# Four PSUM banks for the matrix-building products of a PEER layer, and two weight loads put behind the V rows

## The chip, the cores and the metric

The kernel runs on one NeuronCore of a Trainium2 chip. The time is device microseconds of one execution; what is compared is the median over several runs. Everything is float32 in memory.

## The reference, cut to what matters

Two layers over 256 tokens of width 2048: layer 0 is an mLSTM mixer, layer 1 grouped-query attention, and each is followed by a PEER mixer. The change lies in PEER and in the first load behind it.

```python
def peer(xn, wq, k1, k2, u, v):
    ...                                    # 8 heads, 16 experts each: idx and gate, (tokens, 128)
    def block(args):                       # 2 blocks of 128 tokens
        x_blk, i_blk, g_blk = args
        act = gelu(einsum('td,ted->te', x_blk, u[i_blk]))
        return einsum('te,ted->td', g_blk * act, v[i_blk])

for layer in range(2):
    h = rms_norm(x, ln_mix[layer])
    x = x + (mlstm_mixer, attn_mixer)[layer](h, ...)
    h = rms_norm(x, ln_ffn[layer])
    x = x + peer(h, ...)
```

There are 16384 experts, numbered as 128 x 128. So the second einsum reads, for each token, 128 rows of the table v.

## The kernel before

**PEER's second einsum is done in two ways at once.** Columns 1024 to 2047 of v are gathered: for each token block and each pick p, one indirect DMA brings 128 rows (one per token, 4 KB each, 512 KB in all) and VectorE adds them, scaled, to x (`add_value`, L2001). Columns 0 to 1023 are done dense: `experts_W[b]` is a matrix with, for each expert row e and each token, the weight of the picks on expert (e, partition); 128 expert rows times 2 blocks times 2 banks make 512 matmuls a layer of 128x128 by 128x512 (`dense`, L1433), which gather in PSUM banks acc[0] to acc[3]. The table's half comes in 64 "vd pairs" of 1 MB each, through three slots (`load_dense`, L551, on SP's queue).

**Picks brought forward.** Block 0's first 40 picks are gathered ahead of time ("rows ahead", POOL L631). TensorE adds each with two matmuls against a diagonal matrix (L1418) into acc[0] and acc[1]; VectorE moves these sums to x (L2059) before the dense matmuls of block 0 use the banks. The other gathers (L672, "V rows") are 216 a layer, `G_ALL`, through six slots. The gathers with j under 2 wait for the indices, those with j of 2 and 3 and the vd pair 2 for the last row ahead, and from j = 4 on for the last group of block 1's build.

**The build of `experts_W`.** For each block there are 32 groups of four tokens. For a token t the product of two 128x128 matrices, one-hot by one-hot times weight, gives a 128x128 piece (L1408). Four pieces fill one PSUM bank; TensorE uses `mis[0]` and `mis[1]` in turn. ScalarE copies the bank out (L922). Before group `done` TensorE waits for the copy of the group two before:

```python
if done >= 2:
    pe.wait_ge(wb_out, done - 1)
for j in range(GROUP):
    last = mm(mis[g % 2][:, j * P:(j + 1) * P], onehot_2[g % DEPTH[b]][:, j, :], ...
```

Block 0's build runs beside the dot products with u: ScalarE makes all its selectors (L903) and takes one group at a time. Block 1's build stands by itself, after the last dot product and before the dense phase. In it VectorE makes the weighted selectors of every group (L1981) and the one-hot selectors of the even ones (L1985), ScalarE the one-hot ones of the odd groups (L912, L915); both lie in four buffers, and the selectors of group g wait until group g - 4 is done. ScalarE's order is written out: copies of g and g + 1 (g even), then the selectors for g + 5. Behind the groups 4, 8, ... 24 TensorE adds one row ahead each. I call four groups with one row ahead a round.

**The loads behind.** In layer 0 SP's queue holds, in order, the 64 vd pairs and, put behind the pairs 28, 36, 44 and 52, the four quarters (1 MB each) of the next layer's key weights, chunk 16 of 26 (L510). These go to the arena, where expert rows already used have left room, and VectorE and ScalarE split the first three into two parts between the V rows (L455, L461). Then come the quarters 0 and 1 of chunk 17: quarter 0 into `ring[10]`, once vd pair 62 is used (`vd_used` at 63), quarter 1 into `ring[11]`, a slot of the V rows, once all V rows are added. ScalarE's queue has, behind the build, the load of the next norm's gain (L709, 1 MB), three casts of key quarters, the squares of both x blocks (L721, they wait for all V rows and for the bank sums, L2071), the cast of the fourth quarter and then the casts of the transposed x (L427), on which chunk 16's matmuls wait.

The names of PSUM: eight banks of 512 floats a partition, `acc` = banks 0 to 3, `trb` = 4 and 5 (transposes), `mis` = 6 and 7. acc[2] and acc[3] take block 1's dense sums, and before that mixer chunks.

Of the kernel before, what the change touches and what calls it, by code (L numbers as in the profile page):

```python
# [19 lines left out]
P = 128  # L20
# [68 lines left out]
def trunk_kernel(nc, consts, x, ln_mix, ln_ffn, m_w_in, m_gate_bias, m_head_norm, m_w_out,  # L89
# [13 lines left out]
    CH = 512  # L103
# [9 lines left out]
    with ExitStack() as ctx:  # L113
# [63 lines left out]
        acc, trb, mis = banks[0:4], banks[4:6], banks[6:8]  # L177
# [10 lines left out]
        w_landed = [sem(f"w_landed{j}") for j in range(4)]  # L188
# [29 lines left out]
        wb_full, wb_out = sem("wb_full"), sem("wb_out")  # L218
# [91 lines left out]
        GROUP = 4  # L310
# [8 lines left out]
        spread += [rows_1[:, i * CH:(i + 1) * CH].rearrange("p (t e) -> p t e", e=P) for i in range(4)]  # L319
        onehot_2, weighted_1 = spread[0::2], spread[1::2]  # L320
        DEPTH = [2, 4]

        def wait_spread(eng, l, b, g):

# [181 lines left out]
        def _(sp):  # L506
# [35 lines left out]
            def load_dense(l):  # L542

                for p in range(D_PAIRS):
                    if p == 0:
                        sp.wait_ge(dot_done, (l + 1) * LAYER_TILES)
                    if p == 2:
                        sp.wait_ge(ahead_used, (l + 1) * N_AHEAD)
                    if p >= ND:
                        sp.wait_ge(vd_used, l * D_PAIRS + p - ND + 1)  # L550
                    sp.dma_start(d_slot[p % ND], vd_tab[l][p]).then_inc(vd_landed[p % ND], 16)  # L551
                    if l == 0 and p in KEYS_BEHIND:
                        j = KEYS_BEHIND.index(p)
                        sp.wait_ge(vd_used, 24 + 8 * j)
                        load_quarter(a_w_in[0], slice(4 * CH, 5 * CH), w_raw(16, j), j, keys_landed)
                        sp.sem_inc(w_landed[j], 16)

            KEYS_BEHIND = [28 + 8 * j for j in range(4)]
            load_quarter(m_w_in[0], slice(0, CH), ring[0], 0)
            sp.dma_start(xb[0][:, CH:D], x[0, 0:P, CH:D]).then_inc(x_in[0], 16)  # L560
            sp.dma_start(gain[:, CH:D], ln_mix[0, CH:D].partition_broadcast(P)).then_inc(gain_in, 16)
# [8 lines left out]
            for i, g in enumerate((a_q_norm, a_k_norm)):  # L570
                sp.dma_start(qkgain[:, i * P:(i + 1) * P], g[0].partition_broadcast(P)).then_inc(qkg_in, 16)
            load_dense(0)
            sp.wait_ge(vd_used, D_PAIRS - 1)
            load_quarter(a_w_in[0], slice(5 * CH, 6 * CH), w_raw(17, 0), 0)
            sp.wait_ge(vg_added, G_ALL)
# [126 lines left out]
        def _(act):  # L702
# [151 lines left out]
            def peer(l):  # L854
# [63 lines left out]
                def weights_group(b, g):  # L918

                    act.wait_ge(wb_full, (2 * l + b) * GROUPS + g + 1)  # L920
                    dst = experts_W[b].rearrange("p (q t r) -> p t q r", t=P, r=RUN)[:, GROUP * g:GROUP * (g + 1)]
                    copy(dst, mis[g % 2][:, :].rearrange("p (t q r) -> p t q r", t=GROUP, r=RUN)).then_inc(wb_out, 1)  # L922

                def diagonal(v):

# [176 lines left out]
        def _(pe):  # L1102
# [281 lines left out]
            def peer(l):  # L1384
# [9 lines left out]
                def weights_group(b, g):  # L1394

                    done = (2 * l + b) * GROUPS + g
                    if b == 0:
                        pe.wait_ge(onehot_act, l * (GROUPS + GROUPS // 2) + g + 1)
                    elif g % 2:
                        pe.wait_ge(onehot_act, l * (GROUPS + GROUPS // 2) + GROUPS + g // 2 + 1)  # L1400
                    else:
                        pe.wait_ge(onehot_dve, l * (GROUPS // 2) + g // 2 + 1)
                    if b:
                        pe.wait_ge(weighted_ready, l * GROUPS + g + 1)
                    if done >= 2:
                        pe.wait_ge(wb_out, done - 1)
                    for j in range(GROUP):
                        last = mm(mis[g % 2][:, j * P:(j + 1) * P], onehot_2[g % DEPTH[b]][:, j, :],  # L1408
                                  weighted_1[g % DEPTH[b]][:, j, :],
                                  start=True, stop=True, skip_group_check=True)  # L1410
                    last.then_inc(wb_full, 1)
# [872 lines left out]
```

## Time and profile before

| | us |
|---|---|
| median of 3 runs | 3179.17 (3179.15 to 3181.28) |
| the profiled execution's own time | 3180.36 |
| its span in the profile | 3178.5 |
| TensorE busy | 2229.8 (70%) |
| VectorE busy | 2446.9 (77%) |
| ScalarE busy | 813.8 (26%) |
| GpSimd busy | 1631.3 (51%) |
| DMA | 1096.33 MB, mean 345 GB/s |

How to read it: the rows come from one profiled execution; times are microseconds from the span's start. PE is TensorE's matmuls, PEld its weight loads, DVE VectorE, ACT ScalarE, POOL GpSimd, SPq SyncE's queue. A row of the timeline has the start, the time, the engine, the line of the kernel, the operation, what is written and read, the shapes and a count (xN: neighbouring instructions merged); in brackets the engine's idle time before it and what ended that. A float32 product stands as two records, so x8 is one group and x4 with 128x512 one row ahead. A matmul's end is modelled and overlaps the start of the next.

### The profile page before, as it was taken

To read this page: it belongs to the slowest core of one execution; us is meant where nothing else is said; L and a number is where in the kernel's file an instruction comes from. 1 tells how busy PE (TensorE), PEld (TensorE's weight loads), DVE (VectorE), ACT (ScalarE), POOL (GpSimd) and SP (SyncE) were. 2 spreads that over 40 slices of the span, in tenths; PEclk is the share of its full clock that TensorE was granted. 3 is DMA by queue.
4 is the path that set the end of the run, shared out by engine and by line. 5 is a ranking of instruction groups with operands and counts; after the bars stand their busy time and mean duration, and the time that the engine had idled before them with its cause. 6 is when DMAs were issued, how large, how long until landed. Compare 5 with 4: busy or idle time off the path is not lost.

```text
span 3178.5 us, 23916 instructions
## 1 busy us (share of the span) xinstructions
PE 2229.8 (70%) x7748; PEld 1627.4 (51%) x7748; DVE 2446.9 (77%) x3513; ACT 813.8 (26%) x1773; POOL 1631.3 (51%) x1051
## 2 busy tenths in 40 slices
PE   7999983452134369999989999454213335999999
PEld 6887772341122146666658877343112223666666
DVE  4454579999999986666665767999999998666665
ACT  4344410000345572000003442000025556300000
POOL 1000036657788845655550103556878885365664
PEclk9999996775566679999999999766656767999999
DMA  6554589999999968999984437999999997699998
GB/s 233 179 191 141 181 342 407 421 402 402 417 420 420 420 273 326 413 413 413 412 348 146 159 113 306 405 421 404 413 401 420 420 420 317 263 413 411 413 413 363
DMA packets 231210, 1096.33 MB, mean 345 GB/s; under 512 B 23208, under 2 KB 23984, under 8 KB 144176
## 3 DMA queue, kind: packets, MB, share of 16 engines
q0 software_dynamic: 147456, 805.37, 62.3%
q1 hardware_dynamic: 80256, 282.22, 23.4%
q10 hardware_dynamic: 3376, 7.23, 0.7%
q8 instruction: 62, 1.02, 0.1%
q14 instruction: 60, 0.49, 0.0%
HBM read 1092.63 MB, written 2.11 MB: 344 GB/s over the span
## 4 chain that ended last, share of the span: by engine, by line
PE 34%; DVE 30%; DMA 18%; issue 9%; POOL 7%; ACT 2%; ACTq 0%; SPq 0%; DVEq 0%; POOLq 0%
DVE ring_sb L2027 19%; PE bank L1142 15%; PE bank L1433 14%; DMA actT_sb<-in_peer_vg_dram,idx_all 8%; DMA ring_sb<-in_peer_u_dram,idx_all 6%; POOL ring_sb L655 5%; DMA ring_sb<-in_peer_vg_dram,idx_all 3%; DVE x_sb L2001 1%; PE bank L1408 1%; POOL actT_sb L672 1%; DVE shared L1740 1%; DVE shared L1736 1%; DVE pair_all L1744 1%; PE bank L1418 1%; ACT ring_sb L922 1%
## 5 line engine op out<-in xcount | busy, mean ns | idle before, releaser
L655 POOL DMA_INDIRECT ring_sb<-in_peer_u_dram,idx_all x496 | 889.1, 1792 | 345.1 <-DVE idx_all L1745 203.0
L2027 DVE CUSTOM_DVE_ANT_0 ring_sb<-ring_sb,arena 128x2048 f32<-128x2048 f32 x256 | 574.5, 2286 | 21.9 <-DMA ring_sb<-in_peer_u_dram,idx_all 20.7
L2027 DVE CUSTOM_DVE_ANT_0 ring_sb<-ring_sb,actT_sb 128x2048 f32<-128x2048 f32 x256 | 573.2, 2285 | 13.5 <-DMA ring_sb<-in_peer_u_dram,idx_all 13.1
L2001 DVE SCALAR_TENSOR_TENSOR x_sb<-actT_sb,gate_rows,x_sb 128x1024 f32<-128x1024 f32 x288 | 369.1, 1284 | 222.0 <-DMA actT_sb<-in_peer_vg_dram,idx_all 215.0
L1142 PE MATMUL bank<-w_parts,actT_hi 128*128 128x512 f32 x1664 | 520.8, 394 | 7.3 <-DVE w_parts L461 5.2
L1433 PE MATMUL bank<-ring_sb 128*128 128x512 f32 x1024 | 481.6, 592 | 1.4 <-ACT ring_sb L922 1.4
L1433 PE MATMUL bank<-ring_sb,arena 128*128 128x512 f32 x1024 | 481.3, 593 | 0.4 <-DMA ring_sb<-in_peer_vd_dram 0.4
L672 POOL DMA_INDIRECT actT_sb<-in_peer_vg_dram,idx_all x288 | 349.1, 1212 | 249.0 <-DVE x_sb L2001 190.3
L1408 PE MATMUL bank<-gain 128*128 128x128 f32 x768 | 144.6, 348 | 413.0 <-ACT gain L903 386.9
L1189 PE MATMUL bank<-arena 128*128 128x256 f32 x896 | 249.7, 445 | 233.4 <-DVE shared L2027 233.4
L461 DVE TENSOR_TENSOR w_parts<-ring_sb,w_parts 128x2048 fp32r<-128x2048 f32 x100 | 228.7, 2292 | 212.1 <-ACT w_parts L455 212.1
L1408 PEld LDWEIGHTS bank<-gain 128*128 128x128 f32 x768 | 126.4, 248 | 481.6 <-ACT gain L903 439.0
L1433 PEld LDWEIGHTS bank<-ring_sb,arena 128*128 128x128 f32 x1024 | 301.5, 295 | 139.1 <-DMA ring_sb<-in_peer_vd_dram 2.1
L1433 PEld LDWEIGHTS bank<-ring_sb 128*128 128x128 f32 x1024 | 301.3, 294 | 139.2 <-ACT ring_sb L922 1.7
L1142 PEld LDWEIGHTS bank<-w_parts,actT_hi 128*128 128x128 f32 x1664 | 310.5, 189 | 72.7 <-issue 9.4
L1189 PEld LDWEIGHTS bank<-arena 128*128 128x128 f32 x896 | 200.1, 227 | 280.5 <-DVE shared L2027 245.8
L2001 DVE SCALAR_TENSOR_TENSOR x_sb<-ring_sb,gate_rows,x_sb 128x1024 f32<-128x1024 f32 x144 | 184.3, 1284 | 106.6 <-DMA ring_sb<-in_peer_vg_dram,idx_all 100.8
L1418 PE MATMUL bank<-ring_sb,keysT 128*128 128x512 f32 x272 | 185.8, 825 | 112.4 <-ACT keysT L932 101.8
L455 ACT CAST w_parts<-ring_sb 128x2048 fp32r<-128x2048 f32 x100 | 190.6, 1909 | 273.1 <-DMA ring_sb<-in_mlstm_w_in_dram 134.4
L672 POOL DMA_INDIRECT ring_sb<-in_peer_vg_dram,idx_all x144 | 181.5, 1260 | 152.7 <-DVE x_sb L2001 78.5
L1142 PE MATMUL bank<-w_parts,actT_lo 128*128 128x512 f32 x640 | 249.7, 390 | 0.0
L631 POOL DMA_INDIRECT ring_sb<-in_peer_vg_dram,idx_all x80 | 150.0, 1876 | 78.3 <-PE bank L1418 56.7
(217 smaller groups left out, 2081.1 us busy)
## 6 DMA issues: line engine op xcount, KB each, us to landing
ring_sb<-in_peer_vd_dram SPq DMA_DIRECT2D x128, 1024.0 KB
ring_sb<-in_mlstm_w_in_dram SPq DMA_DIRECT2D x48, 1024.0 KB, 5.1
arena<-in_peer_wq_dram SPq DMA_DIRECT2D x28, 1024.0 KB, 13.7
ring_sb<-in_attn_w_in_dram SPq DMA_DIRECT2D x20, 1024.0 KB, 5.1
ring_sb<-in_mlstm_w_out_dram SPq DMA_DIRECT2D x16, 1024.0 KB, 5.1
ring_sb<-in_attn_w_out_dram SPq DMA_DIRECT2D x16, 1024.0 KB, 5.0
ring_sb<-in_peer_u_dram,idx_all POOLq DMA_INDIRECT x496, 12.8
actT_sb<-in_peer_vg_dram,idx_all POOLq DMA_INDIRECT x288
```

Source lines behind the costliest of these rows:

```text
L455: nc.scalar.copy(w_hi_of[j], w_raw(c, j)).then_inc(w_hi, 1)
L461: nc.vector.tensor_tensor(w_lo_of[j], w_raw(c, j), w_hi_of[j].bitcast(F32), ALU.subtract).then_inc(w_lo[j], 1)
L631: nc.gpsimd.indirect_dma_start(out=ahead_slot[v % 4], out_offset=None, in_=vg_tab[l], in_offset=bass.IndirectOffsetOnAxis(ap=idx_all[0][:, ...
L655: nc.gpsimd.indirect_dma_start(out=ring[i % NU], out_offset=None, in_=u_tab[l], in_offset=bass.IndirectOffsetOnAxis(ap=rows_at, axis=0),). ...
L672: nc.gpsimd.indirect_dma_start(out=g_slot[G_SLOT[j]], out_offset=None, in_=vg_tab[l], in_offset=bass.IndirectOffsetOnAxis(ap=idx_all[b][:, ...
L1142: last = mm(acc[2 * par + b][:, :], xp, wp, start=(j == 0 and k == 0 and i == 0), stop=(j == 3 and k == QK - 1 and i == 2), skip_group_che ...
L1189: last = mm(mis[0][:, side * T:(side + 1) * T], slots[half][:, k % 8, side * P:(side + 1) * P], yT[:, k, :], start=(k == 0), stop=(k == KT ...
L1408: last = mm(mis[g % 2][:, j * P:(j + 1) * P], onehot_2[g % DEPTH[b]][:, j, :], weighted_1[g % DEPTH[b]][:, j, :], start=True, stop=True, s ...
L1418: last = mm(acc[n][:, :], diag_of(v), ahead_slot[v % 4][:, n * CH:(n + 1) * CH], start=(v == 0), stop=(v == N_AHEAD - 1), skip_group_check ...
L1433: last = mm(acc[2 * b + n][:, :], experts_row(b, e), d_slot[p % ND][:, i * DENSE + n * CH:i * DENSE + (n + 1) * CH], start=(e == 0), stop= ...
L2001: v.scalar_tensor_tensor(out=xb[b][:, DENSE:D], in0=g_slot[G_SLOT[j]], scalar=w_all[b][:, p:p + 1], in1=xb[b][:, DENSE:D], op0=ALU.mult, o ...
L2027: v.tensor_tensor_reduce(ring[i % NU], ring[i % NU], rows[b], 1.0, 0.0, ALU.mult, ALU.add, dots[u % 2][:, k:k + 1]).then_inc(dot_done, 1)
```

## The change

A list `built` of four banks takes the place of `mis[g % 2]`: mis[0], mis[1], acc[2], acc[3], and TensorE waits for the copy of the group four before. In layer 0 the last key quarter is no longer put behind vd pair 52 but behind all pairs, and it waits there until 214 of the 216 V rows are added. The first quarter of chunk 17 stands behind it in the same queue, and so behind that wait.

```diff
--- before.py
+++ after.py
@@ -319,6 +319,7 @@
         spread += [rows_1[:, i * CH:(i + 1) * CH].rearrange("p (t e) -> p t e", e=P) for i in range(4)]
         onehot_2, weighted_1 = spread[0::2], spread[1::2]
         DEPTH = [2, 4]
+        built = [mis[0], mis[1], acc[2], acc[3]]
 
         def wait_spread(eng, l, b, g):
 
@@ -555,7 +556,7 @@
                         load_quarter(a_w_in[0], slice(4 * CH, 5 * CH), w_raw(16, j), j, keys_landed)
                         sp.sem_inc(w_landed[j], 16)
 
-            KEYS_BEHIND = [28 + 8 * j for j in range(4)]
+            KEYS_BEHIND = [28 + 8 * j for j in range(3)]
             load_quarter(m_w_in[0], slice(0, CH), ring[0], 0)
             sp.dma_start(xb[0][:, CH:D], x[0, 0:P, CH:D]).then_inc(x_in[0], 16)
             sp.dma_start(gain[:, CH:D], ln_mix[0, CH:D].partition_broadcast(P)).then_inc(gain_in, 16)
@@ -570,6 +571,10 @@
             for i, g in enumerate((a_q_norm, a_k_norm)):
                 sp.dma_start(qkgain[:, i * P:(i + 1) * P], g[0].partition_broadcast(P)).then_inc(qkg_in, 16)
             load_dense(0)
+            sp.wait_ge(vg_added, G_ALL - 2)
+            sp.wait_ge(vd_used, 24 + 8 * 3)
+            load_quarter(a_w_in[0], slice(4 * CH, 5 * CH), w_raw(16, 3), 3, keys_landed)
+            sp.sem_inc(w_landed[3], 16)
             sp.wait_ge(vd_used, D_PAIRS - 1)
             load_quarter(a_w_in[0], slice(5 * CH, 6 * CH), w_raw(17, 0), 0)
             sp.wait_ge(vg_added, G_ALL)
@@ -919,7 +924,7 @@
 
                     act.wait_ge(wb_full, (2 * l + b) * GROUPS + g + 1)
                     dst = experts_W[b].rearrange("p (q t r) -> p t q r", t=P, r=RUN)[:, GROUP * g:GROUP * (g + 1)]
-                    copy(dst, mis[g % 2][:, :].rearrange("p (t q r) -> p t q r", t=GROUP, r=RUN)).then_inc(wb_out, 1)
+                    copy(dst, built[g % 4][:, :].rearrange("p (t q r) -> p t q r", t=GROUP, r=RUN)).then_inc(wb_out, 1)
 
                 def diagonal(v):
 
@@ -1402,10 +1407,10 @@
                         pe.wait_ge(onehot_dve, l * (GROUPS // 2) + g // 2 + 1)
                     if b:
                         pe.wait_ge(weighted_ready, l * GROUPS + g + 1)
-                    if done >= 2:
-                        pe.wait_ge(wb_out, done - 1)
+                    if done >= 4:
+                        pe.wait_ge(wb_out, done - 3)
                     for j in range(GROUP):
-                        last = mm(mis[g % 2][:, j * P:(j + 1) * P], onehot_2[g % DEPTH[b]][:, j, :],
+                        last = mm(built[g % 4][:, j * P:(j + 1) * P], onehot_2[g % DEPTH[b]][:, j, :],
                                   weighted_1[g % DEPTH[b]][:, j, :],
                                   start=True, stop=True, skip_group_check=True)
                     last.then_inc(wb_full, 1)
```

## Rows read from the trace of the kernel before

**Rows 1.** The page, part 2: granted clock and DMA share in 40 slices.

```profile
PEclk9999996775566679999999999766656767999999
DMA  6554589999999968999984437999999997699998
```

**Rows 2.** Busy time by stage: both layers' builds and dense phases.

```profile
core 0: us, PE busy (x) PEld busy (x) DVE busy (x) ACT busy (x) POOL busy (x), PEclk, DMA share, GB/s
1159.26:1212.24 52.98, 43.29 (x280) 35.82 (x280) 46.31 (x144) 43.78 (x108) 6.38 (x7) 0.97 0.27 97
1212.24:1653.21 440.97, 440.58 (x1024) 301.31 (x1024) 274.75 (x214) 5.70 (x3) 260.61 (x212) 1.00 1.02 408
...
2682.45:2735.43 52.98, 44.28 (x280) 36.85 (x281) 46.16 (x143) 43.45 (x107) 6.16 (x7) 0.95 0.27 95
2735.43:3175.27 439.84, 439.84 (x1024) 301.46 (x1024) 274.65 (x217) 0.00 (x0) 262.25 (x212) 1.00 1.00 402
```

**Rows 3.** The timeline at layer 1's end: start us, us, engine, line, instruction.

```profile
3165.45 2.67 DVE L2001 SCALAR_TENSOR_TENSOR x_sb<-actT_sb,gate_rows,x_sb 128x1024 f32<-128x1024 f32 x2 [0.69 <-DMA actT_sb<-in_peer_vg_dram,idx_all]
...
3173.39 1.88 PE L1433 MATMUL bank<-ring_sb 128*128 128x512 f32 x4
```

**Rows 4.** The timeline at layer 0's end, VectorE and ScalarE.

```profile
1655.50 1.28 DVE L2001 SCALAR_TENSOR_TENSOR x_sb<-ring_sb,gate_rows,x_sb 128x1024 f32<-128x1024 f32 x1 [1.68 <-DMA ring_sb<-in_peer_vg_dram,idx_all]
1657.10 2.67 DVE L2001 SCALAR_TENSOR_TENSOR x_sb<-actT_sb,gate_rows,x_sb 128x1024 f32<-128x1024 f32 x2 [0.32 <-DMA actT_sb<-in_peer_vg_dram,idx_all]
...
1664.87 1.88 ACT L455 CAST w_parts<-arena 128x2048 fp32r<-128x2048 f32 x1
...
1668.63 0.58 ACT L427 CAST actT_hi<-bank 128x512 fp32r<-128x512 f32 x1 [1.88 <-PE bank L1115]
```

**Rows 5.** ScalarE's timeline behind it, the next chunk's first cast.

```profile
1692.05 3.72 ACT L455 CAST w_parts<-ring_sb 128x2048 fp32r<-128x2048 f32 x2
```

**Rows 6.** The timeline of one round of the build, layer 0.

```profile
1176.47 0.59 ACT L922 COPY ring_sb<-bank 128x512 f32<-128x512 f32 x1 [1.13 <-PE bank L1408]
...
1179.50 1.13 PE L1408 MATMUL bank<-gain 128*128 128x128 f32 x8 [1.18 <-ACT ring_sb L922]
...
1180.47 1.88 PE L1418 MATMUL bank<-ring_sb,shared 128*128 128x512 f32 x4
1180.67 1.11 DVE L1981 TENSOR_SCALAR gain<-const,shared 128x128 f32<-128x128 f32 x4 [0.43 <-PE bank L1408]
...
1181.58 0.57 ACT L922 COPY ring_sb<-bank 128x512 f32<-128x512 f32 x1
...
1183.08 2.06 PE L1408 MATMUL bank<-actT_sb 128*128 128x128 f32 x16
1183.28 0.59 ACT L922 COPY ring_sb<-bank 128x512 f32<-128x512 f32 x1 [1.13 <-PE bank L1408]
1183.28 1.12 DVE L1981 TENSOR_SCALAR gain<-const,shared 128x128 f32<-128x128 f32 x4 [0.90 <-PE bank L1408]
```

**Rows 7.** TensorE's timeline: starts of the two builds, and layer 0's last four groups.

```profile
1159.26 3.54 PE L1408 MATMUL bank<-gain 128*128 128x128 f32 x16 [2.37 <-DVE gain L1985]
...
1165.87 1.13 PE L1408 MATMUL bank<-gain 128*128 128x128 f32 x8 [1.18 <-ACT ring_sb L922]
...
1206.76 2.02 PE L1408 MATMUL bank<-gain 128*128 128x128 f32 x16 [1.18 <-ACT ring_sb L922]
...
2682.20 3.78 PE L1408 MATMUL bank<-gain 128*128 128x128 f32 x16 [2.38 <-DVE gain L1985]
2685.78 3.09 PE L1408 MATMUL bank<-actT_sb 128*128 128x128 f32 x16
2689.06 1.13 PE L1408 MATMUL bank<-gain 128*128 128x128 f32 x8 [0.19 <-ACT ring_sb L922]
```

**Rows 8.** The DMA issues by line, last column the median us to landing.

```profile
ring_sb<-in_attn_w_in_dram SPq DMA_DIRECT2D x20, 1024.0 KB, 5.1
...
arena<-in_attn_w_in_dram SPq DMA_DIRECT2D x4, 1024.0 KB, 15.9
```

## The prediction

> **What bounds the kernel now.** I read first the profile by slices [rows 1]: the DMA share stands at 9 over two long stretches, and the granted clock is low in between. These stretches are the V phases of the two PEER layers. Then I cut each layer's end into stages [rows 2]. The build of block 1's expert matrix takes 52.98 us, and in it TensorE is busy for 43.29 us, VectorE 46.31, ScalarE 43.78: nobody is full, so they wait for each other. The dense phase behind it takes 440.97 us in layer 0 and 439.84 in layer 1. TensorE is full in it, and so are the DMA engines (share 1.02 and 1.00): two streams side by side, the matmuls with their vd pairs, and the gathered V rows that VectorE adds.
>
> Which of the two ends last differs. In layer 1 the last V row is added at 3165.45 + 2.67 = 3168.12, the last matmul ends at 3173.39 + 1.88 = 3175.27: TensorE ends the layer by 7.15 us [rows 3]. In layer 0 TensorE ends at 1653.21 [rows 2], and the last row is added at 1657.10 + 2.67 = 1659.77 [rows 4]: the V rows end the layer, by 6.56 us. Nothing of what comes next (squares, norm, transposes) starts before that.
>
> **Inside the build.** One round of four groups (16 products of 128x128) and one row ahead [rows 6]. TensorE: a pause of 1.18 us that ends with ScalarE's copy, a group 0.97 (1179.50 to 1180.47), the row ahead and the next group 2.61 (to 1183.08), two groups 2.06: 5.64 us of work in a round of 6.81 (ScalarE's copy at 1176.47 to the next such copy at 1183.28). ScalarE: from 1176.47 to 1181.58 + 0.57 = 1182.15 without a pause, 5.68 us, then 1.13 us idle until TensorE. VectorE waits 0.43 us here and 0.90 at 1183.28, both for TensorE, so it works 5.48. TensorE waits for the copy of the group two before; ScalarE then waits for the group that came late. All three need under 5.7 us; with two banks the round takes 6.81.
>
> **Part 1, four banks in block 1's build.** Group g now waits for the copy of group g - 4. In ScalarE's order the copies of groups 4m and 4m+1 are behind it when TensorE has finished 4m+3, so the pause of 1.18 us goes. No instruction is added: 128 products and 32 copies a layer as before. What is late next is ScalarE's own work, 5.68 us, with TensorE's 5.64 beside it. VectorE's selectors for group g + 4 need only that group g is done, and 5.48 fits. I take 5.75 us a round, a little over the longest of the three; the bounds are 5.68 (no loss) and 6.2 (half of the pause comes back, since three queues in order with nearly the same load can't all run without a gap). From group 4 (1165.87) to group 28 (1206.76) there are six rounds [rows 7]: 6 x 1.06 = 6.4 us. The first round has one pause of that kind, 1.18, before group 4; the queues have only just filled there, so I take 0.7 of it. The last one, 1206.76 to 1212.24 = 5.48 us, becomes two pairs of groups of 2.02 and a copy of 0.57, with the hand-overs about 4.7: 0.7. Layer 0: **7.8 us**, bounds 4.5 and 9.1. In layer 1 the build takes 53.23 us (2682.20 to 2735.43), and its first four groups run at the low clock, 3.78 and 3.09 us for a pair, so that the first pause is 0.19 and not 1.18 [rows 7]: **7.2 us**, bounds 4.0 and 8.1.
>
> Here a page speaks against. The granted clock is 0.97 and 0.95 in the builds [rows 2], that is the high level (2.4 GHz) but for their start, in spite of a pause every round; so I count nothing for the clock. The Trainium skill, "TensorE: Matmul & The Clock Gate", section "A second HAM failure mode: psum-queue depth-cycling", says that a kernel cycling through banks left TensorE small pauses and made its clock swing; by it the build would gain less than the sum or lose. The trace does not agree for two banks, and four take pauses away. It is the last rival.
>
> Block 0's build is paced by ScalarE's selectors, made between the dot products; in its order the copy of group g - 2 stands ahead of the selectors of g. So TensorE never waited for a bank there: zero, and if that cover were gone it would be a gain. Banks 2 and 3 are idle in the build (rows ahead gather in 0 and 1; dense matmuls into 2 and 3 wait for all copies, as they did): zero.
>
> **What the earlier end is worth.** Layer 1: dense phase and V rows both start behind the build, TensorE is without a gap for 439.84 us and ends the layer; all 7.2 us count. Layer 0: the gathers from j = 4 on wait for the last group, the two before and the third vd pair for the last row ahead, both in the build; the V stream moves as a whole, 7.8 us.
>
> **Part 2, two megabytes behind the V rows (layer 0).** Moved are two loads on SP's queue, 1 MB each. The last key quarter leaves its place behind pair 52 and passes 11 vd pairs (53 to 63). The next chunk's first quarter, which waited for vd pair 63 and so went out one pair, 440.97 / 64 = 6.9 us, ahead of TensorE's end, now waits for the last-but-two V row too. The two layers tell what a megabyte costs. Against layer 1, layer 0 carries six more in this phase: the gain for the next norm, four key quarters, the first quarter of chunk 17. Its V rows end 6.56 us behind TensorE, layer 1's 7.15 us ahead: 13.7 / 6 = 2.28 us each. The DMA engines at about 408 GB/s give 1.05 MB / 0.408 = 2.57 us. Two of them out of the V rows' way: **4.6 us**. The row end would stand 2.0 us behind TensorE's, so the V rows still bound the layer; the gain can't pass 6.56 us. The lower bound is 2.0: near the end VectorE adds rows back to back at 1.33 us (two in 2.67) [rows 4] and no free DMA speeds that up. The adds at 1655.50 and 1657.10 waited 1.68 and 0.32 us for their landings, so there is something to win there.
>
> What it could cost. SP now stands at the wait for V row 214; queued behind are only the quarters of chunk 17, the first cast of which is at 1692.05 [rows 5]. The key quarter goes out when row 214 is added, 1655.50 + 1.28 = 1656.78 in the old times. ScalarE casts it at 1664.87, behind the two squares, and the first cast that anybody waits for comes at 1668.63; so it may land until 1668.63 - 1.88 = 1666.75, that is 9.9 us after issue. Median landings are 5.1 us for such loads on a quiet queue and 15.9 for the key quarters in the middle of the dense phase [rows 8]. At 1656.78 the matmuls' loads are over and two V rows are left, so I take a value near 5.1, at most 8: zero cost. If it were 15.9, 6.0 us would be lost.
>
> **The sum.** 7.8 + 7.2 + 4.6 = 19.6 us, on the profiled execution: 3180.4 - 19.6 = 3160.8 us (the span from 3178.5 to 3158.9). The median of the runs lies 1.2 us lower: 3179.2 - 19.6 = **3159.6 us**.
>
> **Rivals.**
> (a) The build gains about half: a round of 6.2, since ScalarE's order (two copies, then a set of selectors) holds up TensorE in another place. For it: three loads of 5.5 to 5.7 us; against: four banks are a slack of a whole round. 4.5 + 4.0 + 4.6 = 13.1: 3166.1 us. Chance 0.12.
> (b) The V rows don't follow the freed megabytes, VectorE being their bound near the end. For it: adds back to back from 1657.10; against: the comparison of the layers. 15.0: 3164.2 us. Chance 0.12.
> (c) The key quarter lands late (15.9 us) and holds up chunk 16: 19.6 - 6.0 = 13.6: 3165.6 us. Chance 0.05.
> (d) The change does not what it says: the bank was only one of two waits that ended together, and TensorE now stops for a selector as long as for the copy. 4.6 us are left: 3174.6 us, no change. Chance 0.03.
> (e) Slower: the clock falls in the build. The first pair of groups at the low level (1.2 GHz) took 3.54 us against 2.02 for a late pair [rows 7], and a stream without pauses would double: 5.64 becomes 11.3, 5.5 us over the 5.75. With four or more of the sixteen rounds low, the 19.6 us are eaten; with all of them it is 16 x 5.5 = 88, some 3248 us. Nothing in the trace shows it: chance 0.02.
>
> **How the numbers follow.** The forecast has 0.66. Its best end is 9.1 + 8.1 + 6.6 = 23.8: 3155.4 us. Its poor end and the rivals (a), (b), (c) lie at up to 3166.1. With half a microsecond to one at either side for the scatter of runs, the range is 3154.5 to 3167. A difference under 0.2%, 6.4 us, can't be told from none: faster 0.95, same 0.03 (d), slower 0.02 (e).
>
> **What would show it.** Right: rounds of 5.7 to 5.8 us and no pause of TensorE for the copy at 1.18; the builds 45 and 46 us long; layer 0's last V row 2 us behind TensorE's last matmul; the key quarter's cast straight behind the squares, with no wait for a DMA; layer 1's dense phase still 440 us. Wrong: a new wait of TensorE for selectors; V rows still 6 us behind; ScalarE waiting for the key quarter; a clock under 1.00 in the middle of a build.

## The result, and the profile after

The changed kernel takes 3158.7 us (median of 4 runs, 3157.0 to 3161.9) against 3179.2 us: 20.5 us less, ratio 0.9931 (95% interval 0.9919 to 0.9942). Forecast were 3159.6. A second set of five runs (e11) gave 0.9922 (0.9909 to 0.9936). The profiled span fell from 3178.5 to 3156.6 us, by 21.9; forecast were 19.6. In the new file the line numbers are up to five higher: the build's products L1413 (were L1408), the copy L927 (L922), the V rows L2006 (L2001), the dense matmuls L1438 (L1433). The files of the experiments differ from this by a few lines again.

First the busy time by stage, the changed kernel (columns as in [rows 2]): the builds and the dense phases of the two layers.

```profile
1160.78:1205.28 44.50, 42.20 (x281) 35.51 (x281) 44.40 (x143) 42.96 (x108) 6.74 (x7) 0.95 0.33 114
1205.28:1647.46 442.18, 442.16 (x1024) 301.47 (x1024) 282.25 (x221) 6.04 (x4) 260.73 (x212) 1.00 1.02 408
2668.71:2713.53 44.82, 42.54 (x280) 35.86 (x281) 44.72 (x144) 42.90 (x108) 6.07 (x7) 0.94 0.33 115
2713.53:3153.37 439.84, 439.84 (x1024) 301.47 (x1024) 275.75 (x217) 0.00 (x0) 268.96 (x212) 1.00 1.00 402
```

The builds take 44.50 and 44.82 us, where they took 52.98 and 53.23 (from the first product to the first dense matmul). TensorE, VectorE and ScalarE are busy for 42.20, 44.40 and 42.96 us, a little less than before (43.29, 46.31 and 43.78), in a time that is 8.5 us shorter. VectorE's 44.40 of 44.50 us is not all selectors: it has made the last of them 3.7 us before the build's end, and goes on with the sums of the rows ahead and the first V rows. Layer 1's dense phase is 439.84 us, as before.

Next TensorE's timeline in layer 0's build, a round in the middle and then the end of the build.

```profile
1177.01 1.06 PE L1413 MATMUL bank<-gain 128*128 128x128 f32 x8
1177.90 1.88 PE L1423 MATMUL bank<-ring_sb,shared 128*128 128x512 f32 x4
1179.62 1.05 PE L1413 MATMUL bank<-gain 128*128 128x128 f32 x8
1180.51 1.95 PE L1413 MATMUL bank<-actT_sb 128*128 128x128 f32 x16
1182.30 1.06 PE L1413 MATMUL bank<-gain 128*128 128x128 f32 x8
...
1200.55 1.16 PE L1413 MATMUL bank<-gain 128*128 128x128 f32 x8 [0.74 <-ACT gain L920]
...
1203.34 1.16 PE L1413 MATMUL bank<-actT_sb 128*128 128x128 f32 x8 [0.74 <-ACT actT_sb L920]
1205.28 3.40 PE L1438 MATMUL bank<-ring_sb 128*128 128x512 f32 x4 [0.78 <-ACT ring_sb L927]
```

and one round of ScalarE's, from an odd group's selectors to those of the group four later:

```profile
1176.24 1.28 ACT L917 ACTIVATE gain<-const,shared 128x128 f32<-128x128 f32 x4
...
1181.82 1.28 ACT L917 ACTIVATE gain<-const,shared 128x128 f32<-128x128 f32 x4
```

A round is 1182.30 - 1177.01 = 5.29 us and has no pause; [rows 6] had 6.81 with 1.18 of pause. ScalarE's round is 1181.82 - 1176.24 = 5.58 us, and from the second group's copy on it never waits again, so it sets the length of the build: TensorE runs ahead of it at 5.29 us a round and from group 20 on goes at 5.58 too. Only at the end does TensorE wait, 0.74 us twice for ScalarE's selectors (L920) and 0.78 for the last copy.

Then layer 0's end, SyncE's queue, VectorE, ScalarE and TensorE.

```profile
1643.07 0.38 SPq L511 DMA_DIRECT2D arena<-in_attn_w_in_dram  x1
1643.15 2.67 DVE L2006 SCALAR_TENSOR_TENSOR x_sb<-actT_sb,gate_rows,x_sb 128x1024 f32<-128x1024 f32 x2
...
1643.57 56.74 SPq L511 DMA_DIRECT2D ring_sb<-in_attn_w_in_dram  x7
...
1645.74 2.48 DVE L2076 TENSOR_TENSOR x_sb<-bank,x_sb 128x512 f32<-128x512 f32 x4
...
1650.91 1.88 ACT L456 CAST w_parts<-arena 128x2048 fp32r<-128x2048 f32 x1
...
1653.53 1.97 PE L1120 MATMUL bank<-const,arena 128*128 128x128 f32 x8 [6.06 <-DVE arena L1642]
1654.68 0.58 ACT L428 CAST actT_hi<-bank 128x512 fp32r<-128x512 f32 x1 [1.88 <-PE bank L1120]
```

and chunk 16's first transposes in the kernel before:

```profile
1667.48 1.75 PE L1115 MATMUL bank<-const,arena 128*128 128x128 f32 x7 [14.27 <-DVE arena L1637]
```

The last V row is added at 1643.15 + 2.67 = 1645.82, 440.54 us after the dense phase's start; before, it was 447.53 [rows 2, 4]. TensorE's last matmul ends at 1647.46: the V rows, 6.56 us late before, are 1.64 us ahead. The key quarter goes out at 1643.07 and is cast at 1650.91 right behind the squares, with no wait for it. TensorE starts on chunk 16's transposes 6.06 us after its last dense matmul, where it was 14.27.

It is still the V rows that release what follows. From the last V row's add to chunk 16's transposes it is 1653.53 - 1645.82 = 7.71 us, and before 1667.48 - 1659.77 = 7.71; all thirteen profiles have 7.70 or 7.71, also the four in which TensorE ends later than the last row (by 1.64 us here, 0.83, 0.17 and 0.05 in e10, e8 and e4). Behind the last V row VectorE adds the four bank sums (L2076), and only the fourth needs TensorE's last matmul: it begins some 1.7 us after the last V row's end (an estimate from the 2.48 us of the four), and in layer 0 no profile shows a wait there. In layer 1 each of the four waits for TensorE:

```profile
3153.41 0.69 DVE L2076 TENSOR_TENSOR x_sb<-bank,x_sb 128x512 f32<-128x512 f32 x1 [0.17 <-PE bank L1438]
```

So in layer 0 TensorE may end up to about 1.7 us behind the last V row before that costs anything, and the change uses 1.64 of them.

By stage, before to after, in us:

| stage | before | after | change |
|---|---|---|---|
| start to layer 0's build | 1159.26 | 1160.78 | +1.5 |
| build, layer 0 | 52.98 | 44.50 | -8.5 |
| dense phase, layer 0 | 440.97 | 442.18 | +1.2 |
| its end to chunk 16 | 14.27 | 6.07 | -8.2 |
| chunk 16 to layer 1's build | 1014.72 | 1015.18 | +0.5 |
| build, layer 1 | 53.23 | 44.82 | -8.4 |
| dense phase, layer 1 | 439.84 | 439.84 | 0 |
| the rest | 3.23 | 3.23 | 0 |

The first line is scatter: nothing there was changed, and the eleven later profiles have it between 1159.1 and 1163.9. The +1.2 is told of at the end; with the -8.2 below it, it makes the 7.0 us by which the last V row comes sooner after the dense phase's start.

### The profile page after: what moved, and what is told of

Read it like the earlier page. It is cut to its first block, busy times and chain, and to the rows that moved or that the text cites. A ratio compares the mean times of both kernels' runs of the same rounds, so it can differ in the third digit from the quotient of the medians.

```text
span 3156.6 us, 23915 instructions
## 1 busy us (share of the span) xinstructions
PE 2231.8 (71%) x7748; PEld 1630.4 (52%) x7748; DVE 2445.7 (77%) x3513; ACT 812.1 (26%) x1773; POOL 1639.5 (52%) x1051
## 4 chain that ended last, share of the span: by engine, by line
PE 33%; DVE 30%; DMA 18%; issue 8%; POOL 7%; ACT 3%; ACTq 0%; SPq 0%; DVEq 0%; POOLq 0%
DVE ring_sb L2032 20%; PE bank L1147 15%; PE bank L1438 14%; DMA actT_sb<-in_peer_vg_dram,idx_all 7%; DMA ring_sb<-in_peer_u_dram,idx_all 6%; POOL ring_sb L660 5%; DMA ring_sb<-in_peer_vg_dram,idx_all 3%; DVE x_sb L2006 2%; ACT ring_sb L927 1%; POOL actT_sb L677 1%; DVE shared L1745 1%; DVE shared L1741 1%; DVE pair_all L1749 1%; POOL ring_sb L636 1%; PE bank L1357 0%
## 5 line engine op out<-in xcount | busy, mean ns | idle before, releaser
L2032 DVE CUSTOM_DVE_ANT_0 ring_sb<-ring_sb,arena 128x2048 f32<-128x2048 f32 x256 | 574.4, 2285 | 21.6 <-DMA ring_sb<-in_peer_u_dram,idx_all 20.3
L2032 DVE CUSTOM_DVE_ANT_0 ring_sb<-ring_sb,actT_sb 128x2048 f32<-128x2048 f32 x256 | 573.4, 2285 | 14.2 <-DMA ring_sb<-in_peer_u_dram,idx_all 13.7
L2006 DVE SCALAR_TENSOR_TENSOR x_sb<-actT_sb,gate_rows,x_sb 128x1024 f32<-128x1024 f32 x288 | 369.0, 1284 | 217.3 <-DMA actT_sb<-in_peer_vg_dram,idx_all 214.1
L1438 PE MATMUL bank<-ring_sb 128*128 128x512 f32 x1024 | 482.9, 594 | 1.5 <-ACT ring_sb L927 1.5
L1438 PE MATMUL bank<-ring_sb,arena 128*128 128x512 f32 x1024 | 481.7, 593 | 0.0
L677 POOL DMA_INDIRECT actT_sb<-in_peer_vg_dram,idx_all x288 | 359.3, 1248 | 233.2 <-DVE x_sb L2006 171.7
L1413 PE MATMUL bank<-gain 128*128 128x128 f32 x768 | 146.1, 351 | 398.6 <-ACT gain L908 386.7
L462 DVE TENSOR_TENSOR w_parts<-ring_sb,w_parts 128x2048 fp32r<-128x2048 f32 x100 | 228.6, 2291 | 214.0 <-ACT w_parts L456 214.0
L1438 PEld LDWEIGHTS bank<-ring_sb,arena 128*128 128x128 f32 x1024 | 301.6, 295 | 139.6 <-issue 1.5
L1438 PEld LDWEIGHTS bank<-ring_sb 128*128 128x128 f32 x1024 | 301.3, 294 | 139.9 <-ACT ring_sb L927 1.9
L1413 PEld LDWEIGHTS bank<-gain 128*128 128x128 f32 x768 | 129.0, 252 | 464.6 <-ACT gain L908 437.3
L2006 DVE SCALAR_TENSOR_TENSOR x_sb<-ring_sb,gate_rows,x_sb 128x1024 f32<-128x1024 f32 x144 | 184.6, 1284 | 102.4 <-DMA ring_sb<-in_peer_vg_dram,idx_all 101.0
```

The costliest lines, as they stand in the source:

```text
L462: nc.vector.tensor_tensor(w_lo_of[j], w_raw(c, j), w_hi_of[j].bitcast(F32), ALU.subtract).then_inc(w_lo[j], 1)
L677: nc.gpsimd.indirect_dma_start(out=g_slot[G_SLOT[j]], out_offset=None, in_=vg_tab[l], in_offset=bass.IndirectOffsetOnAxis(ap=idx_all[b][:, ...
L1413: last = mm(built[g % 4][:, j * P:(j + 1) * P], onehot_2[g % DEPTH[b]][:, j, :], weighted_1[g % DEPTH[b]][:, j, :], start=True, stop=True, ...
L1438: last = mm(acc[2 * b + n][:, :], experts_row(b, e), d_slot[p % ND][:, i * DENSE + n * CH:i * DENSE + (n + 1) * CH], start=(e == 0), stop= ...
L2006: v.scalar_tensor_tensor(out=xb[b][:, DENSE:D], in0=g_slot[G_SLOT[j]], scalar=w_all[b][:, p:p + 1], in1=xb[b][:, DENSE:D], op0=ALU.mult, o ...
L2032: v.tensor_tensor_reduce(ring[i % NU], ring[i % NU], rows[b], 1.0, 0.0, ALU.mult, ALU.add, dots[u % 2][:, k:k + 1]).then_inc(dot_done, 1)
```

## The experiments

Each is compared with the kernel before on the same chip, where that took 3181.1 us (e1 to e4), 3181.6 (e5 to e8) and 3182.2 (e9 to e11). "V end" below is the time from the start of layer 0's dense phase to the last V row's add, read from each profile's timeline. It repeats well: 447.5 and 447.7 us in the two profiles with both loads among the V rows and nothing else moved (before, e1), 440.4 to 441.0 in the six with both loads behind them (the change, e2, e3, e4, e8, e11).

### e1 and e2: one part alone

e1 is the changed kernel with both loads where they were:

```diff
-            KEYS_BEHIND = [28 + 8 * j for j in range(3)]
+            KEYS_BEHIND = [28 + 8 * j for j in range(4)]
...
             load_dense(0)
-            sp.wait_ge(vg_added, G_ALL - 2)
-            sp.wait_ge(vd_used, 24 + 8 * 3)
-            load_quarter(a_w_in[0], slice(4 * CH, 5 * CH), w_raw(16, 3), 3, keys_landed)
-            sp.sem_inc(w_landed[3], 16)
```

> Four banks, both loads where they were before. The changed kernel's builds took 44.5 and 44.8 us instead of 53.0 and 53.2, its V rows ended 7.0 us earlier against the start of the dense phase. Theory 1 (the builds are worth 16.9 us whatever the loads do, the 7.0 us belong to the two megabytes): builds of 44.5 to 45 us, the last V row of layer 0 again 6.6 us behind TensorE's last matmul, 3162 us. Rival (part of the 7.0 us comes from the build, since four banks let the V rows start nearer to the dense phase): the last V row 2 to 5 us behind TensorE, 3157 to 3160 us.

e2 is the kernel before with those lines of the change alone (two banks).

> Two banks, both megabytes behind the V rows. Theory 1: builds of 53 us, the last V row of layer 0 about 1.6 us ahead of TensorE's end, so TensorE ends the layer and 6.6 to 8.2 us are won: 3171 to 3173 us. The prediction's price of 2.28 us a megabyte: last V row 2.0 us behind TensorE's end, 4.6 us won, 3174.6 us. Rival (the V rows did not gain from the loads): last V row 4 us or more behind TensorE, 3177 us or more.

Measured: e1 3165.8 us, ratio 0.9951 (0.9937 to 0.9964); e2 3174.7 us, ratio 0.9979 (0.9970 to 0.9988). VectorE's last V rows and TensorE's last dense matmuls, first e1:

```profile
1644.65 1.88 PE L1434 MATMUL bank<-ring_sb 128*128 128x512 f32 x4
...
1650.50 2.67 DVE L2002 SCALAR_TENSOR_TENSOR x_sb<-actT_sb,gate_rows,x_sb 128x1024 f32<-128x1024 f32 x2 [0.31 <-DMA actT_sb<-in_peer_vg_dram,idx_all]
```

and e2:

```profile
1651.30 2.67 DVE L2005 SCALAR_TENSOR_TENSOR x_sb<-actT_sb,gate_rows,x_sb 128x1024 f32<-128x1024 f32 x2
...
1651.83 1.88 PE L1437 MATMUL bank<-ring_sb 128*128 128x512 f32 x4
```

e1's builds are 44.94 and 45.02 us; its last row ends at 1653.17, 6.64 us behind TensorE (1646.53), V end 447.70. e2's builds are 53.22 us each; its last row ends at 1653.97, 0.26 us behind TensorE (1653.71), V end 440.38. So the builds don't touch the V rows, and the two megabytes alone take 7.1 to 7.3 us from their end. 15.3 us and 6.4 us make 21.7; the change has 20.5 and 24.5 in its two sets. Theory 1 holds in the stages, though e1's 15.3 us is less than the 16.9 expected (its interval is 11.5 to 20.0). e2's 3174.7 us is what the price of 2.28 us had, but its gain of 6.4 us can't tell the two theories apart (interval 3.8 to 9.5). The V rows can: they end 0.26 us behind TensorE and not 2.0, with V end 7.1 us earlier than before, so the prediction's 4.6 was too low.

### e3 and e4: the banks or the wait

```diff
-                    if done >= 4:
-                        pe.wait_ge(wb_out, done - 3)
+                    if done >= 2:                    # e3; in e4: done >= 3
+                        pe.wait_ge(wb_out, done - 1) # e3; in e4: done - 2
```

> The changed kernel with its four banks, but TensorE waits again for the copy of the group two before. Theory (the wait is what costs, not which banks are used): rounds of 6.8 us with a pause of 1.2, builds of 53 us, 17 us slower than the change, 3175 to 3176 us. Rival (spreading the products over other banks itself helps, since writing and copying no longer meet): rounds shorter than 6.5 us, 3170 us or less.

> The changed kernel, TensorE waits for the copy of the group three before. Theory (the round is bound by the loads of the three engines, 5.3 to 5.6 us, and one group of slack is enough): rounds as with four, builds within 0.7 us of the change's, time within 1.5 us of 3158.7. Rival (each bank of slack buys its share of the 8.5 us a build): builds of about 48.8 us, 3167 us.

Measured: e3 3175.2 us, ratio 0.9981 (0.9972 to 0.9990); e4 3158.5 us, ratio 0.9928 (0.9914 to 0.9942). TensorE's timeline, a round of e3:

```profile
1181.58 1.13 PE L1413 MATMUL bank<-gain 128*128 128x128 f32 x8 [1.18 <-ACT ring_sb L927]
1182.54 1.88 PE L1423 MATMUL bank<-ring_sb,shared 128*128 128x512 f32 x4
...
1188.39 1.13 PE L1413 MATMUL bank<-gain 128*128 128x128 f32 x8 [1.18 <-ACT ring_sb L927]
```

and of e4:

```profile
1181.86 1.06 PE L1413 MATMUL bank<-gain 128*128 128x128 f32 x8
1182.75 1.88 PE L1423 MATMUL bank<-ring_sb,shared 128*128 128x512 f32 x4
...
1187.44 1.06 PE L1413 MATMUL bank<-gain 128*128 128x128 f32 x8
```

e3 has four banks in turn and the old round, 1188.39 - 1181.58 = 6.81 us with the old pause of 1.18; its builds are 53.09 and 53.23 us, and its time is e2's. The banks themselves are worth nothing; the wait is. e4's round is 5.58 us, ScalarE's pace, from its third round on, and its builds take 44.93 and 45.41. A wait one group longer lets TensorE run ahead at 5.29 us a round for a while, but the last copy is ScalarE's, and that comes no sooner: one group of slack buys 8 of the 8.4 us, and the builds with the wait four back (44.2 to 45.4 us in the nine profiles that have it) can't be told from e4's.

### e5 and e6: which megabyte

```diff
 # e5: the key quarter alone behind the V rows
             load_dense(0)
+            sp.wait_ge(vd_used, D_PAIRS - 1)
+            load_quarter(a_w_in[0], slice(5 * CH, 6 * CH), w_raw(17, 0), 0)
             sp.wait_ge(vg_added, G_ALL - 2)
...
-            sp.wait_ge(vd_used, D_PAIRS - 1)
-            load_quarter(a_w_in[0], slice(5 * CH, 6 * CH), w_raw(17, 0), 0)
...
 # e6: chunk 17's first quarter alone behind them
-            KEYS_BEHIND = [28 + 8 * j for j in range(3)]
+            KEYS_BEHIND = [28 + 8 * j for j in range(4)]
...
             load_dense(0)
             sp.wait_ge(vg_added, G_ALL - 2)
-            sp.wait_ge(vd_used, 24 + 8 * 3)
-            load_quarter(a_w_in[0], slice(4 * CH, 5 * CH), w_raw(16, 3), 3, keys_landed)
-            sp.sem_inc(w_landed[3], 16)
```

> The changed kernel, but only the key quarter behind the V rows; chunk 17's first quarter again goes out one vd pair ahead of TensorE's end. From the dense phase's start to the last V row it was 447.6 us with both loads among the V rows and 440.5 with both behind. Theory 2 (a megabyte in the full stretch costs its transfer, 2.6 us, and one in the tail more, since there the last gathers have no others behind them that could catch up): 447.6 - 2.6 = 445.0, the last V row 4 to 5 us behind TensorE, 3162 us. Rival (every megabyte costs the same, 3.5 us): 444.1 us. Rival (the key quarter is all of it): 440.5 us.

> The changed kernel, but only chunk 17's first quarter behind the V rows; the key quarter again behind vd pair 52. Theory 2: the quarter in the tail was worth 7.1 - 2.6 = 4.5 us, so 443.1 us from the dense phase's start to the last V row, which stands 2 us behind TensorE's end, and 3160 to 3161 us. Rival (the same price for each): 444.1 us. Rival (it was hidden in the tail anyway): 447.6 us and 3165 us.

Measured: e5 3162.1 us, ratio 0.9936 (0.9920 to 0.9953); e6 3161.5 us, ratio 0.9938 (0.9922 to 0.9955). VectorE's third split (L462, behind row 202) and last V row, e5:

```profile
1625.74 2.28 DVE L462 TENSOR_TENSOR w_parts<-arena,w_parts 128x2048 fp32r<-128x2048 f32 x1
...
1649.43 1.28 DVE L2006 SCALAR_TENSOR_TENSOR x_sb<-actT_sb,gate_rows,x_sb 128x1024 f32<-128x1024 f32 x1 [1.36 <-DMA actT_sb<-in_peer_vg_dram,idx_all]
```

and e6:

```profile
1627.57 2.29 DVE L462 TENSOR_TENSOR w_parts<-arena,w_parts 128x2048 fp32r<-128x2048 f32 x1
...
1646.45 2.67 DVE L2003 SCALAR_TENSOR_TENSOR x_sb<-actT_sb,gate_rows,x_sb 128x1024 f32<-128x1024 f32 x2
```

The dense phases start at 1208.96 and 1205.09. I set the five cases side by side, all in us from the dense phase's start: the time of the third split, which is when 202 rows are done, V end, and the difference of the two.

| key quarter | chunk 17's first | run | third split | V end | the last stretch |
|---|---|---|---|---|---|
| among | among | e1 | 423.0 | 447.7 | 24.7 |
| behind | among | e5 | 416.8 | 441.8 | 25.0 |
| among | behind | e6 | 422.5 | 444.0 | 21.6 |
| behind | behind | change | 416.8 | 440.5 | 23.8 |
| two more in the middle | behind | e7 | 429.0 | 451.0 | 22.0 |

Of what was expected, e6 fits equal prices (444.1), but e5's 441.8 fits nothing. The key quarter alone is worth 5.9 us and the other alone 3.7, together 7.2: they don't add. The key quarter takes 6.2 us from the time of row 202 with the other among the rows, 5.7 with it behind; the other profiles with both behind (e2, e3, e4, e8, e11) have 416.7 to 417.3 there and the kernel before 422.8. The other one acts only in the last stretch, where it saves 3.1 us with the key quarter among the rows (24.7 to 21.6) and 1.2 without (25.0 to 23.8).

### e7: two more megabytes in the middle

```diff
+                    if l == 0 and p in (40, 48):
+                        j = 1 if p == 40 else 2
+                        sp.wait_ge(keys_landed[j], 16)
+                        load_quarter(a_w_in[0], slice(4 * CH, 5 * CH), w_raw(16, j), j, keys_landed)
...
-                    act.wait_ge(keys_landed[j], 16)
+                    act.wait_ge(keys_landed[j], 32 if j in (1, 2) else 16)
```

> The changed kernel with two more megabytes in the middle of layer 0's dense phase: key quarters 1 and 2 are loaded a second time behind vd pairs 40 and 48. If a megabyte there costs its transfer at 408 GB/s (theory 2), the V rows end 5.1 us later, 445.6 us after the dense phase's start and 3 to 4 us behind TensorE, 3162 us. If it costs 3.5 us each: 447.5 us. Rival (the prediction's 2.28 us): 445.1 us. If VectorE and not the DMA engines bounded the V rows: 440.5 us and no change of time.

Measured: 3164.7 us, ratio 0.9943 (0.9926 to 0.9959), with V end at 451.0, later than any of the theories had it. Busy time in stretches of e7, columns as in [rows 2]: the dense phase up to vd pair 35, to the first split, and the last stretch.

```profile
1205.42:1445.40 239.98, 239.97 (x559) 164.48 (x560) 149.95 (x118) 1.91 (x1) 144.05 (x120) 1.00 1.02 411
1445.40:1566.43 121.03, 121.03 (x284) 83.06 (x283) 65.35 (x52) 3.80 (x2) 55.26 (x52) 1.00 1.02 411
1634.39:1656.41 22.02, 11.09 (x26) 7.11 (x25) 20.17 (x17) 0.00 (x0) 12.26 (x9) 0.84 0.81 273
```

and the same for the changed kernel:

```profile
1205.28:1445.30 240.02, 240.02 (x555) 163.50 (x556) 149.89 (x119) 1.90 (x1) 144.13 (x120) 0.99 1.02 411
1445.30:1555.76 110.46, 110.44 (x258) 75.49 (x257) 65.27 (x51) 3.80 (x2) 59.64 (x52) 1.00 1.02 412
1622.06:1645.82 23.76, 23.76 (x57) 16.41 (x56) 20.18 (x17) 0.00 (x0) 13.07 (x9) 1.00 0.94 361
```

The first stretch is the same. The second takes 121.03 us instead of 110.46, at the same 411 to 412 GB/s: two megabytes at that rate are 5.1 us, and 10.6 were lost. V end is 450.99, 10.4 us later. So a megabyte in the middle costs 5.2 us, twice its transfer, and that is a dose of the same thing as the key quarter's 6.2. A part of the reason may lie in the rates; this is worked out, not tested. While TensorE runs it takes a vd pair every 6.9 us (440 / 64), which is 1.05 MB / 6.9 us = 152 GB/s. V rows get only what is left, 411 - 152 = 259 GB/s, and a megabyte is 4.0 us of that (an estimate from these rows): in the time in which the V rows are held up the matmuls' loads go on. In the end all bytes must come, and one would think that the last stretch gives back what was paid too much, for in e7 the vd pairs are over there. It can't: VectorE needs 14 adds at 1.34 us and a split of 2.3, 21.0 us, in any case, and the last row of the table stands at 22.0 with the DMA engines at 0.81. Between 4.0 and the measured 5.2 to 6.2 us a remainder stays open.

### e8: the key quarter last

```diff
             sp.wait_ge(vg_added, G_ALL - 2)
-            sp.wait_ge(vd_used, 24 + 8 * 3)
-            load_quarter(a_w_in[0], slice(4 * CH, 5 * CH), w_raw(16, 3), 3, keys_landed)
-            sp.sem_inc(w_landed[3], 16)
             sp.wait_ge(vd_used, D_PAIRS - 1)
             load_quarter(a_w_in[0], slice(5 * CH, 6 * CH), w_raw(17, 0), 0)
             sp.wait_ge(vg_added, G_ALL)
             load_quarter(a_w_in[0], slice(5 * CH, 6 * CH), w_raw(17, 1), 1)
+            sp.wait_ge(vg_added, G_ALL - 2)
+            sp.wait_ge(vd_used, 24 + 8 * 3)
+            load_quarter(a_w_in[0], slice(4 * CH, 5 * CH), w_raw(16, 3), 3, keys_landed)
+            sp.sem_inc(w_landed[3], 16)
```

> The changed kernel with the key quarter last of the three loads behind the V rows, after both quarters of chunk 17. In the changed kernel it went out 7.8 us ahead of its cast, and no engine waited. Here it goes out 2.7 us later and behind two megabytes (5.1 us at 408 GB/s). Theory (the place had only 2 to 4 us to spare): ScalarE waits for it ahead of chunk 16's casts, 2 to 5 us slower than the change, 3161 to 3164 us. Rival (it has time enough in any place): 3158.7 us.

Measured: 3160.5 us, ratio 0.9936 (0.9919 to 0.9952). The timeline of SyncE's queue, TensorE and ScalarE:

```profile
1647.05 0.45 SPq L511 DMA_DIRECT2D arena<-in_attn_w_in_dram  x1
...
1654.25 1.97 PE L1121 MATMUL bank<-const,arena 128*128 128x128 f32 x8 [7.54 <-DVE arena L1643]
1654.49 1.90 ACT L456 CAST w_parts<-arena 128x2048 fp32r<-128x2048 f32 x1 [2.76 <-DMA arena<-in_attn_w_in_dram]
1656.30 1.07 ACT L428 CAST actT_hi<-bank 128x512 fp32r<-128x512 f32 x2
```

It goes out at 1647.05 and ScalarE, free at 1651.73, waits 2.76 us for it: it landed about 7.4 us after its issue, behind 2 MB. The casts of the transposed rows come at 1656.30, 2.05 us after the transposes began, where the changed kernel had 1.15 (1653.53 to 1654.68). So 2.8 us of wait cost 0.9. The expected 2 to 5 us did not come; the time of 3160.5 can't be told from the change's. In its place in the change the key quarter had 7.84 us from issue to cast and nobody waited: rival (c) of the prediction is ruled out there, and even two megabytes in front of it cost less than 1 us.

### e9 to e11: the splits earlier, and the change again

```diff
-            KEYS_SPLIT = [G_ALL - 46, G_ALL - 30, G_ALL - 14]
+            KEYS_SPLIT = [G_ALL - 54, G_ALL - 38, G_ALL - 22]
```

> Four banks, both loads among the V rows (as in e1, where the V rows end layer 0), but VectorE splits the first three key quarters eight V rows earlier each, before rows 162, 178 and 194 instead of 170, 186 and 202. Theory 3 (near the end VectorE bounds the V rows: the last split of 2.3 us and the last 14 rows take 21.5 to 25 us in every run, whatever the DMA engines have to spare, so a split taken out of this stretch is won): from the dense phase's start to the last V row 445.4 us instead of 447.7, 2.3 us faster than e1. Rival (the DMA engines bound the V rows to the end): 447.7 us, no change against e1.

> The changed kernel with the same earlier splits. Its last V row stood 1.6 us ahead of TensorE's last matmul in one profile, level with it in the run that waits for three. Theory 3: the last V row 2 to 4 us ahead of TensorE, but TensorE ends the layer now, so between 0 and 1.5 us faster than the change. Rival (the V rows still bound the layer): 2.3 us faster.

> The changed kernel once more, to be compared with the two above and with its own first profile. In that one the granted clock fell to 0.50 for some 3 us at the start of layer 0's dense phase, behind the last groups of the build, and the dense phase took 442.2 us instead of 440 to 441. If that belongs to the change, it is here again; if it comes now and then, as in one of the two layers of e8 alone among the other four-bank runs, most likely not. 20 to 22 us faster than the kernel before.

Measured: e9 3165.3 us, ratio 0.9946 (0.9933 to 0.9960); e10 3158.6 us, 0.9925 (0.9912 to 0.9939); e11 3157.6 us, 0.9922 (0.9909 to 0.9936). e9's VectorE in its last 20 us, what it waited for:

```profile
DVE x_sb L2002 <- DMA actT_sb<-in_peer_vg_dram,idx_all: 3.2, 3, 2.2
DVE x_sb L2002 <- DMA ring_sb<-in_peer_vg_dram,idx_all: 2.7, 1, 2.7
```

e9's row 202 is added 2.5 us earlier than e1's (420.6 to 423.1), but V end is 446.6, only 1.1 earlier: the rest became waits for landings (5.9 us here). In e10 nothing of the 2.3 us is won: its V end is 441.4, the change's 440.5 and e11's 440.6. Row 202 is added at 417.7, no earlier than with the late split, and the waits for landings behind it come to 4.6 us. So theory 3 is at most half right with the loads among the rows, and wrong for e10, where the V rows' end was set by when the gathers landed (one profile each). In time e9 can't be told from e1, nor e10 from e11: no version was found that beats the change. e10's last row ends 0.83 us ahead of TensorE and not 2 to 4, e11's 0.33 behind. The expectation's "TensorE ends the layer now" is not borne out either: chunk 16's transposes start 7.70 us after the last V row in both.

## Why the prediction was right

**The bound.** Both stages were read rightly: TensorE ends layer 1, the V rows ended layer 0, and what the builds lost was a wait and not work. e3 shows that it was the wait for the copy two before. In e1 the builds alone gain 15.3 us of time (11.5 to 20.0), in its stages 16.2.

**Part 1, the builds.** Forecast were 7.8 and 7.2 us; measured 8.5 and 8.4, within the bounds of 9.1 and 8.1 in layer 0 and 0.3 over them in layer 1. Two terms were mis-sized, in opposite ways:

| part of layer 0's build | forecast gain | measured |
|---|---|---|
| first round, to group 4 | 0.7 | 6.61 - 5.65 = 1.0 |
| six rounds, group 4 to 28 | 6.4 | 40.89 - 32.33 = 8.6 |
| last stretch, group 28 to the end | 0.7 | 5.48 - 6.52 = -1.0 |

The round of 5.75 was 5.29 at first and then 5.58. I took the last record's full length into ScalarE's 5.68 and TensorE's 5.64, though the next instruction starts before the recorded end, and I allowed a loss for three queues in order, of which nothing was to be seen. And I treated the last stretch as if TensorE's products were what is left there. ScalarE is the longest of the three, so TensorE's lead of five rounds at 5.29 is given back: it waits twice for ScalarE's selectors (0.74 us each, which the prediction had named as a sign of being wrong) and 0.78 for the last copy, and the "hand-overs about 4.7" took 6.52. The sum came out near because what counts is ScalarE's work from start to end, and its round of 5.58 is not far from 5.75. In layer 1 the first round's pause was 0.19 us only, as said; there the start at the low clock was shorter this time, 2.60 us for the second pair of groups instead of 3.09, and these 0.5 us of the 8.4 are not the change's.

**The page that spoke against.** The prediction set the Trainium skill's section "A second HAM failure mode: psum-queue depth-cycling" ("TensorE: Matmul & The Clock Gate") against the granted clock of the builds. With four banks the builds stand at 0.95 and 0.94, as before at 0.97 and 0.95, and their middle at 1.00: in the builds the clock did not swing. What came instead is in the last section.

**Part 2, the loads.** Forecast were 4.6 us, from 2.28 us a megabyte; measured are 7.0 to 7.2. The step that failed is the price: the difference of the two layers, 13.7 us, was divided evenly among six megabytes. The two that were moved are worth 7.0 us together; the four that stayed come to the rest, 440.5 us of V end in layer 0 against 433.3 in layer 1, or 1.8 us each. Yet the two that e7 added in the middle cost 5.2 us each. So the price depends on place and company: 5 to 6 us where vd pairs flow beside the load, 1 to 4 behind the last of them, and why the four that stayed come out so cheap stays open. The forecast that the row end "would stand 2.0 us behind TensorE's" was wrong: it stands between 1.6 ahead and 0.5 behind in the seven profiles with both loads behind and none added. That the V rows still bound the layer was right even so, by the 7.71 us from the last row to chunk 16 in every profile. And "the gain can't pass 6.56 us" was wrong, since TensorE's end has those 1.7 us of room: 7.0 us came through, and the estimate for the most that could is 6.56 + 1.7 = 8.2. The zero for the key quarter's later place was right (e8).

**The sum.** 8.5 + 8.4 + 7.0 = 23.9 us by the stages, less 1.5 + 0.5 of scatter in stages that nothing touched, is the 21.9 of the span; the medians give 20.5. All five rivals are out: the rounds are shorter than 5.75 (a), the V rows followed (b), the key quarter's place cost nothing (c), TensorE's waits for selectors are 1.5 us a build (d), and the clock held in the middle of the builds (e). The two parts were both forecast too low, by 4.3 us together. That 3159.6 came within 0.9 us of the median is luck: 2.0 us went in stages that nothing touched and 1.4 more from the profiles to the medians. In the second set (e11) the change gains 24.5 us, and against that the forecast of 19.6 is 5 us short.

## What to carry to other kernels

When three engines with equal loads hand a buffer round, look for the pause that comes back each round, and let the wait reach one buffer further back: here that bought nearly everything, and only the wait, not the choice of banks, counted (a build with three banks was not run). What bounds the stage then is the longest of the three engines from its first to its last instruction, not a round of the one that used to pause. A load put among transfers that somebody waits for may cost more than its own transfer: 5.2 to 6.2 us here against 2.6, and bytes over the rate that the other stream leaves (4.0 us) explain only a part of it. Move it behind the last such transfer, and check the time from its issue to its first use. When two streams end close together, find what each of them releases before you say which one ends the stage: here the work behind needs the matmuls 1.7 us later than the rows.

## What was not expected of the hardware

The clock fell after the build, in some runs. TensorE pauses 0.74, 0.74 and 0.78 us at the end of the four-bank build, and in the changed kernel's first profile the granted clock then went to 0.50 for some 3 us (columns as in [rows 2]):

```profile
1203.00:1205.00 2.00, 1.16 (x8) 0.97 (x8) 2.00 (x2) 2.00 (x5) 0.00 (x0) 1.00 0.00 0
1205.00:1207.00 2.00, 1.72 (x3) 1.07 (x4) 2.00 (x3) 0.23 (x1) 1.60 (x2) 0.73 0.78 246
1207.00:1209.00 2.00, 2.00 (x3) 0.78 (x3) 0.79 (x1) 0.00 (x0) 1.39 (x3) 0.50 1.12 297
1209.00:1211.00 2.00, 2.00 (x5) 1.18 (x4) 0.00 (x0) 0.00 (x0) 1.70 (x2) 0.92 0.78 303
```

The dense phase took 442.18 us instead of 440.1 to 441.1. The first four records took 3.40 us there and 2.09 before. The same came in e10's layer 0 (442.19) and e8's layer 1 (441.53 against 439.84), behind none of the other seventeen builds that wait for the copy three or four groups before, and behind none of the six with the old wait, whose last pauses were of the same kind (0.77 and 0.68). The dense phase is 1.1 to 2.1 us longer by it in layer 0 and 1.7 in layer 1. In layer 1, where TensorE ends the layer, that is lost; in layer 0 the V rows hide it, for the changed kernel's V end is 440.54 with the fall and 440.57 without it (e11). Whether the change makes it likelier can't be told from so few.
